# Banded attention in a two-layer block kernel: mask, scale, maximum and sink in one VectorE operation

## What is computed

```python
# 512 tokens in 4 query blocks of 128; 8 query heads, 2 key/value heads, head size 64
scores = einsum(q_block, k_of_the_block_before_this_and_after) * 64 ** -0.5
scores = where(|k_pos - q_pos| <= 128 and 0 <= k_pos < 512, scores, -inf)
mx     = maximum(max(scores, axis=-1), sink)
p      = exp(scores - mx)
denom  = sum(p) + exp(sink - mx)
out    = (p / denom) @ v
```

## Time and profile before

| what | value |
|---|---|
| time, median of 3 runs | 1011.54 us (1010.75 to 1012.36) |
| span of the profiled execution, first to last instruction | 1007.1 us |
| PE busy | 965.1 us (96%), 5224 products |
| weight loads | 814.3 us (81%) |
| DVE busy | 490.0 us (49%), 804 instructions |
| ACT busy | 474.1 us (47%) |
| POOL busy | 449.8 us (45%) |
| DMA | 84.07 MB, mean 83 GB/s |

### The profile page before, as it was taken

How to read it: one execution, slowest core, us unless ns; L and a number is a source line. 1 busy time by engine, 2 the same in 40 slices (tenths; PEclk the granted TensorE clock), 3 DMA queues, 4 the chain that set the end, 5 groups by cost and what they waited for, 6 DMA issues and landing times.

```text
span 1007.1 us, 12885 instructions
## 1 busy us (share of the span) xinstructions
PE 965.1 (96%) x5224; PEld 814.3 (81%) x5224; DVE 490.0 (49%) x804; ACT 474.1 (47%) x831; POOL 449.8 (45%) x255
## 2 busy tenths in 40 slices
PE   8999898899999999999989989999999999999997
PEld 6987667799999997887867768888888888888886
DVE  4066884677776372524265442533333332564444
ACT  6565387665652362544666532633333333342233
POOL 4555356730003543444685822545345435363440
PEclk9999899999999999999999999999999999999999
DMA  9512210000002045224222121332322322333212
GB/s 341 186 62 83 84 42 1 1 1 1 2 4 82 1 158 169 93 82 128 75 65 82 63 63 63 106 104 95 114 85 86 115 92 84 105 105 105 85 41 84
DMA packets 25306, 84.07 MB, mean 83 GB/s; under 512 B 3008, under 2 KB 3264, under 8 KB 25120
## 3 DMA queue, kind: packets, MB, share of 16 engines
q1 hardware_dynamic: 24240, 81.88, 24.7%
q10 hardware_dynamic: 1008, 1.38, 0.4%
HBM read 79.06 MB, written 2.10 MB: 81 GB/s over the span
## 4 chain that ended last, share of the span: by engine, by line
PE 79%; DVE 10%; ACT 6%; POOL 2%; issue 2%; DMA 1%; SPq 0%; ACTq 0%; DVEq 0%
PE bank L1960 76%; PE bank L1968 3%; DVE qk L1512 2%; DVE vc L1512 1%; ACT wh L1165 1%; POOL wl L1045 1%; ACT L1165 1%; DVE mp L1506 1%; DVE r L1506 1%; POOL qk L1056 1%; DVE xf L1506 1%; ACT qk L1165 1%; DMA xt<-in_xt 1%; ACT ee L1165 1%; ACT sl L1165 1%
## 5 line engine op out<-in xcount | busy, mean ns | idle before, releaser
L1045 POOL TENSOR_TENSOR wl<-raw,wh 128x1024 fp32r<-128x1024 f32 (+1 forms) x130 | 312.0, 2405 | 373.1 <-ACT wh L1165 373.1
L1960 PE MATMUL bank<-xh,wh 128*128 128x512 f32 (+1 forms) x536 | 207.2, 387 | 3.4 <-POOL wl L1045 2.3
L1960 PE MATMUL bank<-xh,wl 128*128 128x512 f32 (+1 forms) x536 | 205.3, 383 | 0.0
L1960 PE MATMUL bank<-xl,wh 128*128 128x512 f32 (+1 forms) x536 | 205.2, 383 | 0.0
L1165 ACT ACTIVATE wh<-raw 128x1024 fp32r<-128x1024 f32 (+2 forms) x132 | 135.9, 1036 | 132.1 <-PE bank L1960 124.9
L1960 PE MATMUL bank<-wh,xh 128*128 128x512 f32 (+1 forms) x352 | 141.5, 402 | 9.0 <-POOL wl L1045 3.8
L1960 PE MATMUL bank<-wh,xl 128*128 128x512 f32 (+1 forms) x352 | 135.6, 385 | 0.0
L1960 PE MATMUL bank<-wl,xh 128*128 128x512 f32 (+1 forms) x352 | 135.3, 384 | 0.0
L1960 PEld LDWEIGHTS bank<-xh,wh 128*128 128x128 f32 x536 | 100.8, 188 | 24.2 <-DVE qk L1512 3.1
L1960 PEld LDWEIGHTS bank<-xh,wl 128*128 128x128 f32 x536 | 100.7, 188 | 20.0
L1960 PEld LDWEIGHTS bank<-xl,wh 128*128 128x128 f32 x536 | 100.8, 188 | 19.1
(11 more groups left out here) (256 smaller groups left out, 1590.7 us busy)
## 6 DMA issues: line engine op xcount, KB each, us to landing
raw<-in_wflat SPq DMA_DIRECT2D x126, 512.0 KB, 3.5
xt<-in_xt SPq DMA_DIRECT2D x8, 256.0 KB, 4.4
h<-in_x SPq DMA_DIRECT2D x4, 512.0 KB, 8.0
h<-in_x SPq DMA_DIRECT2D x1, 2048.0 KB, 8.3
gain<-in_pr SPq DMA_DIRECT2D x3, 512.0 KB, 3.6
consts<-in_cf SPq DMA_DIRECT2D x1, 1472.0 KB, 11.6
raw<-in_wflat SPq DMA_DIRECT2D x4, 272.0 KB, 12.0
kh<-kh SPq DMA_DIRECT2D x8, 128.0 KB, 2.3
```

Source lines behind the costliest of these rows:

```text
L1045: e.tensor_tensor(WL[u % NS][:, 0:n], RAW[u % NS][:, 0:n], WH[u % NS][:, 0:n].bitcast(F32), ALU.subtract).then_inc(w_lo.up(u), 1)
L1960: return e.matmul(o, l, r_, start=start, stop=stop, skip_group_check=part)
```

## The change

The bf16 mask products go. A float32 tile `M3` of 128 x 384 holds the lower mask, zeros and the upper mask side by side; block 0 reads it from column 128 on, the others from column 0. One DVE operation, tensor_tensor_reduce, reads the scores in bank 5 and `M3`, writes (score + mask) * -0.125 to `PM[n % 2]` in SBUF, and gives the minimum of that row and the negated sink as `MX`. ACT's exponential then reads and writes `PM[n % 2]` in place with scale -1. So bank 5 is free when DVE has read it, and PE's S(n) waits for that of piece n-1 and no longer for ACT; the wait for the turning of piece n-2 moves from ACT to DVE. `NLb` goes, `NUb` stays (the second block uses it). PE's wait for the identity tile ahead of S(0) goes.

```diff
@@ Dry
-    activation = tensor_tensor = tensor_scalar = scalar_tensor_tensor = tensor_reduce = issue
+    tensor_tensor_reduce = activation = tensor_tensor = tensor_scalar = scalar_tensor_tensor = tensor_reduce = issue
@@ program
-    NLb = sb("nlb", [128, 128], BF16, C0 + 20.5)
+    M3 = sb("m3", [128, 384], F32, C0 + 21)
@@
-    emptied[5], emptied[6], emptied[7] = (swa_a, ("p", 31)), (swa_a, ("pt", 31)), (swa_v, ("o", 3))
+    emptied[5], emptied[6], emptied[7] = (swa_v, ("mx", 31)), (swa_a, ("pt", 31)), (swa_v, ("o", 3))
@@ scalar_engine, swa_s
             on.wait_ge(*swa_v.at(("mx", n)))
-            if n > 1:
-                on.wait_ge(*swa_p.at(("t", n - 2)))
-            act(PM[n % 2][:, 0:nk], psum[5][:, 0:nk], ACT.Exp, swa_a.up(("p", n)), bias=MX[:, qb, h:h + 1], scale=0.125,
+            act(PM[n % 2][:, 0:nk], PM[n % 2][:, 0:nk], ACT.Exp, swa_a.up(("p", n)), bias=MX[:, qb, h:h + 1], scale=-1.0,
                 accum_out=DEN[:, qb, h:h + 1])
@@ vector_engine, masks
             ts(NUb[:], cf("SU"), NEG, None, ALU.mult, const_set.up("nu"))
-            ts(NLb[:], cf("SL"), NEG, None, ALU.mult, const_set.up("nl"))
+            ts(M3[:, 0:128], cf("SL"), NEG, None, ALU.mult, const_set.up("m3a"))
+            e.memset(M3[:, 128:256], 0.0).then_inc(const_set.up("m3b"), 1)
+            ts(M3[:, 256:384], cf("SU"), NEG, None, ALU.mult, const_set.up("m3"))
@@ vector_engine, swa_s
+            nk = swa_keys(qb)[1]
+            at = 0 if qb else 128
             on.wait_ge(*swa_p.at(("s", n)))
-            e.tensor_reduce(mx, psum[5][:, 0:swa_keys(qb)[1]], AX.X, ALU.max, negate=True).then_inc(swa_v.up(("m0", n)), 1)
-            on.wait_ge(*swa_v.at(("m0", n)))
             on.wait_ge(*const_set.at("nsink"))
-            ts(mx, mx, 0.125, NSINK[:, h:h + 1], ALU.mult, swa_v.up(("mx", n)), ALU.min)
+            if n > 1:
+                on.wait_ge(*swa_p.at(("t", n - 2)))
+            e.tensor_tensor_reduce(PM[n % 2][:, 0:nk], psum[5][:, 0:nk], M3[:, at:at + nk], -0.125, NSINK[:, h:h + 1], ALU.add, ALU.min,
+                                   accum_out=mx).then_inc(swa_v.up(("mx", n)), 1)
@@ tensor_engine, swa_s
             if n:
-                on.wait_ge(*swa_a.at(("p", n - 1)))
+                on.wait_ge(*swa_v.at(("mx", n - 1)))
                 p = psum[5]
             else:
                 p = bank(("swa", 5))
                 on.wait_ge(*rope_v.at(("lo", 4, 1)))
-                on.wait_ge(*const_set.at("id"))
-            masks = ([(0, NLb)] if qb > 0 else []) + ([(nk - 128, NUb)] if qb < 3 else [])
             for K, last in ((KHH[g], False), (KLL[g], True)):
-                mm(p[:, 0:nk], QHL[h][:, qb * 128:(qb + 1) * 128], K[:, k0 * 128:k0 * 128 + nk], not last, last)
-            for at, mask in masks:
-                t = mm(p[:, at:at + 128], IDb[:], mask[:], False, True, True)
+                t = mm(p[:, 0:nk], QHL[h][:, qb * 128:(qb + 1) * 128], K[:, k0 * 128:k0 * 128 + nk], not last, last)
             t.then_inc(swa_p.up(("s", n)), 1)
```

## The result

The changed kernel took 1031.5 us (median of four executions: 1029.3, 1031.0, 1032.1 and 1075.0) against 1011.2 us before. The forecast was 1007.1 us, so it was wrong in sign. The same kernel, measured again beside the experiments in four more sittings on four chips, gave about 1007 us more often than 1030: of 31 executions in all, 16 took 1003.1 to 1009.3 us (median 1006.9), 11 took 1027.2 to 1032.1 us, and 4 took 1074.5 to 1076.6. None of 97 executions of the kernel before, run beside the experiments, took over 1013.2 us.

A forecast was written before the change was run, and what follows sets the result against it. It took a short DVE-bound start, then a long PE-bound stretch; masks 2.1, waits 0.3, DVE 0.75, start 1.2 and S(0)'s masks 0.1 sum to 4.4 us, so 1011.5 - 4.4 = 1007.1 us, range 1005.0 to 1010.2.

The forecast's parts named there:

- the clock term: PE's clock, at half for 3.4 us after a wait: work shifted against such a stretch wins or loses about 1.7 us.
- (d): Rival: DVE's new operation slowed by sharing its read of `M3` with POOL at the start; 3.0 us slower, 1014.5 us, chance 0.05.
- The step before it: At query blocks' ends PE arrives earlier and only waits longer for `swo`; only DVE's 0.25 us each counts, 0.75 us in all.
- Mask products: 48 products off PE, priced by distance of starts at 0.06 us for one, 0.10 for a pair; 2.1 us won.
- the 0.55 that was counted: Between O(8) and O(24): 0.25 us from DVE's shorter work and 0.3 us from S(n) no longer waiting for ACT's exponential.
- DVE: Two DVE operations become one: 0.25 us saved per piece, counted at three ends as 0.75 us.
- full rate: DVE's new operation runs one element per cycle, like a copy from PSUM; half rate would add 0.28 or 0.42 us.
- rival (a): The reduction costs a second DVE instruction, so a piece saves 0.12 us instead of 0.25; 1007.8 us, chance 0.17.
- The start: S(3) freed from ACT's exponential, T(2) 1.6 us earlier, then a bank limits PE; 1.2 us won, ends 0.5 and 1.6.
- Edits at nothing: DVE's new wait for the turning, ACT reading SBUF, added constants and the dropped identity wait cost or win nothing.
- Sum: 2.1 + 0.3 + 0.75 + 1.2 + 0.1 = 4.4 us, subtracted from the 1011.5 us median: 1007.1 us.
- The chances: Faster 0.84, the same 0.11, slower 0.05; the forecast of 1007.1 us itself 0.56.

The follow-up runs named there:

- e2: The changed kernel with the 48 bf16 mask products put back on PE; median 1008.3 us, 0.998 of the kernel before, none of ten fell.
- e3: The kernel before with its 48 mask products left out, nothing else changed; four of nine took 1030.8 to 1031.3 us, the others 1005.7 to 1007.8.
- e10: The changed kernel run again unaltered, beside the kernel before; all four executions fell, 1028.5 to 1029.4 us, ratio 1.018.
- e1: The changed kernel itself, run again; three of ten fell (1074.5, 1029.1, 1027.2 us), the others took 1003.1 to 1009.3 us, ratio 0.997.
- e13_after_third: The changed kernel a third time, unaltered; one of four fell (1029.3 us), the profiled execution kept its clock at 1007.0 us.

## Why the prediction was wrong

**The step that failed** is the clock term at the end of the sum: "a shift of the work against such a stretch can win or lose about 1.7 us". The clock was priced by one stretch of 3.4 us, which lies at 544 us among products of up to 512 columns, and as a stretch that is there already and only shifts. The runs showed a new fall, and one that lasts: half clock held 51 or 150 us, up to the inversion's seventh level. That term measures 23 us (a mean of 1029.7 us for the 11 short falls, against 1006.5) or 69 us (1075.4 us for the 4 long ones). No rival had it; the slower one (d), sharing with POOL, did not come about: its operation takes at most 0.62 us.

**The step before it had the trigger and threw it away.** "PE comes to these places earlier too, so it only waits longer": the longer wait was counted as no loss, since it hides what would have been won. It went from 0.44 to 0.99 us and from 0.68 to 0.94, in a stage of small products. That these waits start the fall is the likeliest reading, as said above, and not proved.

**Mask products.** The distance of starts was the right kind of price, and set too low: O(8) to O(24) won 2.7 us where 0.25, 0.3 and some 1.5 of masks were counted. Taken apart by e2 and e3, the masks of this stretch cost 1.7 to 2.2 us, and the rest, 0.54 us beside the masks, is the 0.55 that was counted. That taking products off PE can also cost it the clock was not counted.

**DVE.** 0.18 us saved a piece, not 0.25; full rate, as taken. The second instruction of rival (a) exists and holds nothing, so its sum was wrong too.

**The start.** 1.3 us forecast (1.2, and 0.1 for S(0)), 1.3 measured, and that is partly luck. S(3) is freed as forecast, but the working let T(2) come 1.6 us earlier and had a bank hold PE behind it; in the run T(2) itself waits 0.38 us for ACT's copy of piece 1, and there is no wait for a bank in this place.

**Edits at nothing.** DVE's new wait and the constants show no price. The exponential from SBUF takes 616 ns for 384 columns, against 582 ns from PSUM in the kernel before.

**Sum.** 4.4 us forecast, 5.2 measured within the stage and 4.0 in the whole time of the executions that kept their clock (mean of 16: 1006.5 us; of 97 before: 1010.5). The 4.4 us between span and median of the kernel before were not all outside the span: in the executions measured later the time is 1.8 to 2.0 us above the span, so that profiled execution was itself some 2.5 us faster than the median. The forecast did not rest on it.

**The chances.** 0.05 for slower, where about half of the executions are slower by 16 us or more, and in two of five sittings all four were.

## What to carry to other kernels

Before taking work off a PE that is busy with small products, look where it waits, and ask whether it will reach that wait earlier. If the clock falls there, the price is not that of the pause but of all the work from there to the place where the clock comes back, and a short stretch of half clock elsewhere in the trace does not give it: here 3.4 us in two places, 51 and 150 us in the two that mattered. A single profile in which the clock held does not tell how near it was to falling, so run such a kernel many times, on more than one chip, and read the granted clock of each execution. The best version found moves the waiting step back in the order, behind one more inversion step (1.09 us of products): 1006.4 us, 0.995 to 0.996 of the kernel before, with no fall in 12, where 4 of 13 of the changed kernel fell beside it.

## What the runs showed of the hardware

- PE's clock fell to 1.2 GHz 0.5 to 1.5 us after waits of 0.95 to 0.99 us, in a stretch where PE had been 98 to 100% busy with products of 64 to 384 columns (75.64 of 77 us in e10, 23.00 of 23 us in e1), and stayed there for 51.2 or 150 us while PE was busy throughout. It came back in the same work each time, 5.1 to 5.8 us after the first product of the inversion's seventh level. The Trainium skill (TensorE: Matmul & The Clock Gate, "A second HAM failure mode: psum-queue depth-cycling") tells of small idles between groups of products that make the clock go down and up by turns. Near 199 us it did go down and up, within 3.4 us; from 230 or 284 us on it went down once and stayed for 150 or 51 us.
- A pause of PE of 4.2 or 4.5 us in the same stretch made the clock fall in all of eight executions, 2.2 and 3.7 us after PE had stopped, and it stayed at half for 160.4 or 54.6 us, in which PE was 99% busy.
- The same program fell in 3 of 10, 4 of 4, 1 of 4, 3 of 9 and 4 of 4 executions of five sittings.
- An operation of DVE that adds, scales, writes a tile and reduces takes 477 ns for 256 and 612 ns for 384 columns from PSUM, and its accumulator read of 81 ns overlaps the next operation entirely (e13_after_third).
